# Sliding-window attention in a fused three-block kernel: two key blocks' probabilities in one 128x128 tile

## The chip, the cores and the metric

One core of a Trainium2 chip runs one program. The metric is device microseconds (us) of one execution, as the median of several. The engines are named as in the profile: PE is TensorE's matrix product, PEld its weight load, DVE is VectorE, ACT ScalarE, POOL GpSimd, SP SyncE.

## The reference, cut to what matters

The program is three transformer blocks in a row on 512 tokens of width 1024. The change is in the second block's mixer, an attention in which each 128-query block sees its own key block and the one before it, but only the last 128 keys:

```python
rel = QBLK + a_idx - j_idx                 # a: query in its block, j: key in the 256 of two blocks
def block(args):
    ...
    valid = (rel >= 0) & (rel < C_WINDOW) & (key_pos >= 0)     # C_WINDOW = 128
    bias = jnp.where(valid, alibi, MASK_VALUE)                 # -slope * rel, or -1e30
    s = jnp.einsum('bqhgd,bkhd->bhgqk', qi, kb) * scale + bias
    m = jnp.maximum(jnp.max(s, axis=-1, keepdims=True), sink)
    p = jnp.exp(s - m)
    denom = jnp.sum(p, axis=-1, keepdims=True) + jnp.exp(sink - m)
    return jnp.einsum('bhgqk,bkhd->bqhgd', p / denom, vb)
```

There are 16 query heads of 64 columns on 2 key/value heads. Query a of a block sees key j of its own block where j <= a, and key j of the block before where j > a. So of every two keys with the same number j exactly one is seen.

## The kernel before

Everything is fp32, products of activations and weights are made of three products of rounded parts (hi and lo). `c_stage` of each engine holds the second mixer. It takes the 16 heads as 8 pairs (m = 0, 1 is the head in the pair) and each pair in two rounds r of two query blocks (b = 0, 1; i = 2(r % 2) + b is the query block), 16 rounds in all. Every engine runs its own instruction stream in the written order, and they meet by semaphores only. The order of work is a loop over r in each engine's `c_stage`, with 18 iterations, since the steps of a round are spread over three of them:

- PE, iteration r: `scores(r)` (products of queries and keys to PSUM), `fill(r)` (12 of the products of the next projection's weights, line 1295, which need nothing of the attention), `turn(r-1)` (transposes of the probability tiles of the round before, line 1355), every second iteration a small product for the query norm, and `values(r-2)` (line 1372, transposed probabilities against the value tokens `vtok`).
- DVE, iteration r: `finish(r-1)` (line 2304 takes the reciprocal of the row sums, line 2309 multiplies the tiles by it, in place, and releases `turn` by `c_fin`), `maxima(r)` (line 2295: negative score plus bias into the probability tile, and its row minimum), in odd iterations `scaled` (line 2273, the queries of the next pair, on which the next `scores` waits), in even ones `output` (line 2320, the low part of the finished head pair), then evacuations of `fill`'s banks and `lo_piece` (line 2249, the low part of the weights that `fill` uses later).
- ACT, iteration r: the norm's logarithm and exponential in odd iterations (`norm_job`), or `high` (line 1704) in even ones, `exps(r)` (line 1691, four exponentials with row sums, one for each head and query block), `copy(r-1)` (line 1700, transposed tiles from PSUM to SBUF), `hi_piece` (line 1661, the high part of weights), and in four iterations `square_high` (line 1682).

Two of the waits cross the loops. `lo_piece`'s first half waits until both halves of `hi_piece` are done, and the second of these stands in the same iteration (r = 1, 5, 11, 15), behind `copy(r-1)`. `square_rest` (line 2316, DVE, at the head of iterations 1, 5, 7 and 11) waits for `square_high`, which stands at the end of ACT's iteration before.

A probability tile is 320 columns wide in memory: 256 of keys (block i-1, then block i; for i = 0 only the second 128 are used) and one column with the sink's negative logit, which the exponential adds to the row sum. The lines that the change touches in `turn` and `values`:

```python
for b, i, w in c_blocks(r):                # w = 128 for i = 0, else 256
    for j in range(256 - w, 256, P):
        last = pe.transpose(psum[:, 6 + m, 256 * b + j:256 * b + j + P], c_prob(m, r, b)[:, j:j + P], ident)
```

So `turn` makes 6 transposes for an even round and 8 for an odd one, and `values` one product for each seen key block, head and query block: 14 for a pair (each shows as two records).

## Time and profile before

| what | us |
|---|---|
| median of 3 runs | 1877.54 (1877.28 to 1877.8) |
| the profiled execution | 1877.37 |
| its span on the core | 1875.6 |
| the attention rounds, 578.4 to 680.0 of the span | 101.6 |

The page gives busy time for each engine and the chain of work that ended last. In a timeline row the first number is the start in the span, the second the time from the start of the row's first instruction to the end of its last; a row may hold several instructions (x8) that overlap. What stands in square brackets is how long the engine had sat idle before and what ended that. Instruction durations overlap the next one's start a little, so four in a row take less than four times one.

### The profile page before, as it was taken

How to read it: one execution, taken by the hardware profiler on the slowest of the kernel's cores; microseconds unless marked ns; L12 is line 12 of the kernel's file. 1: busy time of each engine (PE TensorE's matmuls, PEld its weight loads, DVE VectorE, ACT ScalarE, POOL GpSimd, SP SyncE). 2: the span in 40 equal slices, each digit the busy share in tenths (PEclk: the TensorE clock that was granted, in tenths of full speed). 3: DMA queues.
4: the chain of work that ended last, by engine and by line, in shares of the span. 5: the costliest groups of instructions: out<-in, count | busy, mean ns of one | idle time of the engine just before them, and what ended most of it. 6: DMA issues, size and time to landing. Idle time of an engine off the chain costs nothing.

```text
span 1875.6 us, 24415 instructions
## 1 busy us (share of the span) xinstructions
PE 1861.8 (99%) x8998; PEld 1497.4 (80%) x8998; DVE 1189.6 (63%) x1841; ACT 794.4 (42%) x1197; POOL 148.0 (8%) x108
## 2 busy tenths in 40 slices
PE   8999999999999999999999999999999999999999
PEld 6767888888887788888888887888777788888887
DVE  5786677357647866763566498675666667743762
ACT  5365443133435754342334343422577544322441
POOL 2022000000021010000000101121211010000000
PEclk9999999999999999999999999999999999999999
DMA  6212222322231122223232322435333122223222
GB/s 218 70 62 70 92 89 76 114 102 89 84 106 57 51 85 90 89 90 112 90 103 74 125 90 92 142 131 181 137 130 113 68 91 89 80 99 113 90 78 101
DMA packets 39105, 185.99 MB, mean 99 GB/s; under 512 B 4416, under 2 KB 5312, under 8 KB 24432
## 3 DMA queue, kind: packets, MB, share of 16 engines
q1 hardware_dynamic: 38736, 184.77, 28.8%
q8 instruction: 49, 0.80, 0.2%
q14 instruction: 32, 0.26, 0.0%
q10 hardware_dynamic: 288, 0.16, 0.0%
HBM read 176.42 MB, written 8.49 MB: 99 GB/s over the span
## 4 chain that ended last, share of the span: by engine, by line
PE 94%; DVE 4%; ACT 1%; issue 0%; DMA 0%; DVEq 0%; SPq 0%; ACTq 0%
PE banks L760 55%; PE banks L1295 22%; PE banks L807 5%; PE banks L837 1%; PE banks L1209 1%; PE banks L1234 1%; PE banks L1220 1%; PE banks L1343 1%; DVE w_lo L1996 1%; PE banks L1372 1%; DVE tmp L2390 1%; PE banks L1355 1%; PE banks L1308 1%; ACT w_hi L1449 1%; PE banks L969 1%
## 5 line engine op out<-in xcount | busy, mean ns | idle before, releaser
L760 PE MATMUL banks<-xn_hi,w_hi 128*128 128x512 f32 x1208 | 468.4, 391 | 0.2 <-DVE big L2088 0.2
L760 PE MATMUL banks<-xn_hi,w_lo 128*128 128x512 f32 x1208 | 466.1, 389 | 0.0
L760 PE MATMUL banks<-xn_lo,w_hi 128*128 128x512 f32 x1208 | 466.0, 389 | 0.0
L1449 ACT ACTIVATE w_hi<-raw 128x2048 fp32r<-128x2048 f32 (+2 forms) x134 | 228.3, 1703 | 228.4 <-PE banks L760 190.0
L1996 DVE TENSOR_TENSOR w_lo<-raw,w_hi 128x2048 fp32r<-128x2048 f32 (+2 forms) x134 | 273.6, 2042 | 48.5 <-ACT w_hi L1449 48.0
L760 PEld LDWEIGHTS banks<-xn_hi,w_hi 128*128 128x128 f32 x1208 | 226.7, 188 | 49.1 <-issue 1.8
L760 PEld LDWEIGHTS banks<-xn_lo,w_hi 128*128 128x128 f32 x1208 | 226.8, 188 | 48.0 <-issue 1.2
L760 PEld LDWEIGHTS banks<-xn_hi,w_lo 128*128 128x128 f32 x1208 | 226.7, 188 | 47.4
L1511 ACT ACTIVATE tmp<-scaled_h,par 128x512 f32<-128x512 f32 x132 | 100.6, 809 | 349.9 <-DVE scaled_h L2046 349.8
L2046 DVE TENSOR_TENSOR scaled_h<-banks,token_rs 128x512 f32<-128x512 f32 x132 | 85.1, 686 | 186.2 <-PE banks L760 165.9
L1295 PE MATMUL banks<-xn_hi,w_hi 128*128 128x512 f32 x400 | 161.2, 403 | 0.6 <-DVE big L2096 0.6
L1295 PE MATMUL banks<-xn_lo,w_hi 128*128 128x512 f32 x400 | 158.8, 397 | 0.0
L1295 PE MATMUL banks<-xn_hi,w_lo 128*128 128x512 f32 x400 | 158.6, 396 | 0.0
L760 PE MATMUL banks<-hid_hi,w_hi 128*128 128x512 f32 x396 | 154.0, 389 | 0.0
L760 PE MATMUL banks<-hid_lo,w_hi 128*128 128x512 f32 x396 | 154.0, 389 | 0.0
L760 PE MATMUL banks<-hid_hi,w_lo 128*128 128x512 f32 x396 | 154.0, 389 | 0.0
L2019 DVE TENSOR_TENSOR x<-banks,x 128x512 f32<-128x512 f32 (+1 forms) x47 | 32.5, 692 | 169.1 <-PE banks L760 150.9
L659 POOL TENSOR_TENSOR sq<-sq 128x512 f32<-128x512 f32 x38 | 58.4, 1538 | 845.2 <-ACT sq L1455 833.7
L2054 DVE SCALAR_TENSOR_TENSOR tmp<-scaled_h,par,tmp 128x511 f32<-128x511 f32 x132 | 98.8, 748 | 34.9 <-ACT tmp L1511 34.9
L2058 DVE SCALAR_TENSOR_TENSOR tmp<-scaled_h,par,tmp 128x510 f32<-128x510 f32 x132 | 99.1, 750 | 14.5 <-DVE tmp L2054 12.4
L2249 DVE TENSOR_TENSOR w_lo<-raw,w_hi 128x1024 fp32r<-128x1024 f32 (+2 forms) x59 | 81.2, 1379 | 38.4 <-ACT w_hi L1661 38.4
L1295 PEld LDWEIGHTS banks<-xn_hi,w_hi 128*128 128x128 f32 x400 | 75.1, 188 | 28.8 <-issue 13.3
(288 smaller groups left out, 2626.4 us busy)
## 6 DMA issues: line engine op xcount, KB each, us to landing
raw<-weights SPq DMA_DIRECT2D x114, 1024.0 KB, 4.8
raw<-weights SPq DMA_DIRECT2D x24, 768.0 KB, 4.4
raw<-weights SPq DMA_DIRECT2D x24, 640.0 KB, 3.9
big<-scratch SPq DMA_DIRECT2D x40, 256.0 KB, 4.4
att<-scratch SPq DMA_DIRECT2D x16, 256.0 KB, 4.3
scratch<-stage SPq DMA_DIRECT2D x12, 256.0 KB, 4.4
scratch<-con SPq DMA_DIRECT2D x12, 256.0 KB, 2.2
raw<-weights SPq DMA_DIRECT2D x5, 512.0 KB, 3.8
```

The source lines that it names most:

```text
L659: pool.tensor_tensor(chunk(sq, 0), chunk(sq, 0), chunk(sq, c), ALU.add).then_inc(sq_summed, 1)
L760: return pe.matmul(psum[:, 2 * p + m, :], w[:, at_:at_ + P], x_part(k), start=start, stop=stop)
L807: return pe.matmul(psum[:, 2 * (s % 2), :], w[:, at_:at_ + P], x_part(k), start=(k == 0 and t == 0), stop=(k == k_n - 1 and t == 2))
L1295: ins = pe.matmul(c_bank(u), w[:, at_:at_ + P], x_part(k), start=(k == 0 and t == 0), stop=(k == k_n - 1 and t == 2))
L1449: act.activation(w_hi[:, sl], raw[:, sl], ACT.Identity).then_inc(hi_done, 1)
L1511: act.activation(chunk(tmp, 2 * j + m), chunk(scaled_h, 2 * j + m), ACT.Identity, bias=pcol(conv_b, c), scale=pcol(conv, 3 * c + 2)).then_ ...
L1996: dve.tensor_tensor(w_lo[:, sl], raw[:, sl], w_hi[:, sl].bitcast(F32), ALU.subtract).then_inc(lo_done, 1)
L2019: last = dve.tensor_tensor(chunk(x, c), psum[:, 2 * ((a + j) % 2) + m, :], chunk(x, c), ALU.add)
L2046: dve.tensor_tensor(chunk(scaled_h, 2 * j + m), psum[:, 2 * ((a + j) % 2) + m, :], token_rs[:, :], ALU.mult).then_inc(h_scaled, 1)
L2054: me.mark(dve.scalar_tensor_tensor(out=chunk(tmp, t, 1), in0=bank[:, 0:T - 1], scalar=pcol(conv, 3 * c + 1), in1=chunk(tmp, t, 1), op0=ALU ...
L2058: dve.scalar_tensor_tensor(out=chunk(tmp, t, 2), in0=bank[:, 0:T - 2], scalar=pcol(conv, 3 * c), in1=chunk(tmp, t, 2), op0=ALU.mult, op1=A ...
L2249: ins = dve.tensor_tensor(w_lo[:, sl], raw[:, sl], w_hi[:, sl].bitcast(F32), ALU.subtract)
```

## The change

The two key blocks' scores of one query block are put into one 128-column tile by an elementwise minimum (the tile holds negative scores, and a masked key has +1e30, so the minimum picks the seen one of each two keys): `c_pack`, line 2321 in the new file, for the query blocks with i > 0. The exponential, the division and the transpose then work on 128 columns each. In the transposed tile the rows j <= a belong to the own block. The product with the values becomes: whole tile times the values of the block in front, plus (tile times the triangle mask `tri`) times the difference of values between the own block and the one in front. The differences are computed once (`v_diff`, line 2363) before the rounds; the masked copy once a round and head (`masked`, line 2333), behind the rest of DVE's iteration. For i = 0 only the whole tile times the own block's values is needed.

The division moves from DVE to ACT (`normed`, line 1706), at the head of ACT's iteration; DVE keeps the reciprocal.

```diff
         def c_prob(m, r, b):
             return att[:, bass.ds(7 * T + 320 * (4 * (r % 2) + 2 * b + m), 320)]
+        v_diff = chunk(att, 3)
+        def c_packs(r, m, b):
+            return 6 * (r // 2) + (m + 1 if r % 2 == 0 else 2 + 2 * m + b + 1)
...
-                        for b, i, w in c_blocks(r):
-                            for j in range(256 - w, 256, P):
-                                last = pe.transpose(psum[:, 6 + m, 256 * b + j:256 * b + j + P], c_prob(m, r, b)[:, j:j + P], ident)
+                        for b in range(2):
+                            last = pe.transpose(psum[:, 6 + m, b * P:(b + 1) * P], c_prob(m, r, b)[:, P:2 * P], ident)
                         last.then_inc(c_pt, 1)
...
                     pe.wait_ge(c_copied, 2 * r + 2)
+                    pe.wait_ge(c_masked, 2 * r + 2)
                     for b, i, w in c_blocks(r):
-                        first = max(i - 1, 0)
-                        for j in range(first, i + 1):
+                        parts = [(vtok[0], max(i - 1, 0), b * P)] + ([(v_diff, i - 1, (2 + b) * P)] if i else [])
+                        for n, (v, j, from_) in enumerate(parts):
                             for m in range(2):
                                 at_ = j * P + 64 * m
-                                from_ = 256 * b + 256 - w + (j - first) * P
-                                last = pe.matmul(psum[64 * m:64 * m + 64, 2, i * P:(i + 1) * P], vtok[0][:, at_:at_ + 64],
+                                last = pe.matmul(psum[64 * m:64 * m + 64, 2, i * P:(i + 1) * P], v[:, at_:at_ + 64],
                                                  c_slot(m, r)[:, from_:from_ + P],
...
                 def exps(r):
-                    n = 4 * r
                     for m in range(2):
                         for b, i, w in c_blocks(r):
-                            n += 1
-                            act.wait_ge(c_max, n)
-                            pr = c_prob(m, r, b)[:, 256 - w:257]
+                            if i:
+                                act.wait_ge(c_pack, c_packs(r, m, b))
+                            else:
+                                act.wait_ge(c_max, 4 * r + 2 * m + 1)
+                            pr = c_prob(m, r, b)[:, P:2 * P + 1]
...
+                def normed(r):
+                    act.wait_ge(c_inv, r + 1)
+                    for m in range(2):
+                        for b, i, w in c_blocks(r):
+                            pr = c_prob(m, r, b)[:, P:2 * P]
+                            last = act.activation(pr, pr, ACT.Identity, scale=row_inv[:, 2 * i + m:2 * i + m + 1])
+                        last.then_inc(c_fin, 1)
+
                 def copy(r):
...
-                        act.activation(c_slot(m, r)[:, c0:T], psum[:, 6 + m, c0:T], ACT.Identity).then_inc(c_copied, 1)
+                        act.activation(c_slot(m, r)[:, 0:2 * P], psum[:, 6 + m, 0:2 * P], ACT.Identity).then_inc(c_copied, 1)
...
                 for r in range(C_ROUNDS + 2):
+                    if 1 <= r <= C_ROUNDS:
+                        normed(r - 1)
...
+                    for m in range(2):
+                        dve.wait_ge(c_max, 4 * r + 2 * m + 2)
+                        for b, i, w in c_blocks(r):
+                            if i:
+                                pr = c_prob(m, r, b)
+                                dve.tensor_tensor(pr[:, P:2 * P], pr[:, 0:P], pr[:, P:2 * P], ALU.min).then_inc(c_pack, 1)
 
                 def finish(r):
                     n = 4 * (r % 2)
                     dve.wait_ge(c_exp, 4 * r + 4)
-                    me.mark(dve.reciprocal(row_inv[:, n:n + 4], row_sum[:, n:n + 4]))
-                    me.wait()
+                    dve.reciprocal(row_inv[:, n:n + 4], row_sum[:, n:n + 4]).then_inc(c_inv, 1)
+
+                def masked(r):
+
+                    b0 = 1 - r % 2
                     for m in range(2):
-                        for b, i, w in c_blocks(r):
-                            pr = c_prob(m, r, b)[:, 256 - w:256]
-                            last = dve.tensor_scalar(pr, pr, row_inv[:, 2 * i + m:2 * i + m + 1], None, ALU.mult)
-                        last.then_inc(c_fin, 1)
+                        dve.wait_ge(c_copied, 2 * r + m + 1)
+                        dve.tensor_tensor(c_slot(m, r)[:, (2 + b0) * P:T].rearrange("p (j l) -> p j l", j=2 - b0),
+                                          c_slot(m, r)[:, b0 * P:2 * P].rearrange("p (j l) -> p j l", j=2 - b0),
+                                          ccol("tri", 0, P).rearrange("p (o l) -> p o l", o=1).to_broadcast([P, 2 - b0, P]), ALU.mult).then_inc(c_masked, 1)
...
+                dve.wait_ge(c_v, 1)
+                dve.tensor_tensor(v_diff[:, 0:3 * P], vtok[0][:, P:T], vtok[0][:, 0:3 * P], ALU.subtract).then_inc(c_v, 1)
                 for r in range(C_ROUNDS + 2):
...
                             lo_piece(s + 1, r - g0 - 1, 2)
+                    if 1 <= r <= C_ROUNDS:
+                        masked(r - 1)
```

The change also moves instructions. DVE at the end of iteration 11 and the start of iteration 12, before (lines 2295, 2273, 2277, 2264, 2249, 2304, 2309 are the maxima, the next queries, the bias, an evacuation, the low part of weights, the reciprocal, the division):

```order
L2295 ISA att,small<-banks,att,small 128x256
L2295 ISA small 128x1
L2273 SCALAR_TENSOR_TENSOR att<-big,small,rsk 128x512
L2277 TENSOR_SCALAR att<-con 128x256
L2264 TENSOR_TENSOR x<-banks,x 128x512
L2249 TENSOR_TENSOR w_lo<-raw,w_hi 128x1024
L2304 RECIPROCAL small<-small 128x4
L2309 TENSOR_SCALAR att<-att,small 128x256 x4
```

The same place in the changed program (2321 is the pack, 2265 the low part of weights, 2333 the masked copy):

```order
L2311 ISA att,small<-banks,att,small 128x256
L2311 ISA small 128x1
L2321 TENSOR_TENSOR att<-att 128x128 x4
L2289 SCALAR_TENSOR_TENSOR att<-big,small,rsk 128x512
L2293 TENSOR_SCALAR att<-con 128x256
L2280 TENSOR_TENSOR x<-banks,x 128x512
L2265 TENSOR_TENSOR w_lo<-raw,w_hi 128x1024
L2333 TENSOR_TENSOR att<-att,con 128x128 x2
L2326 RECIPROCAL small<-small 128x4
```

Four packs now stand between the maxima and the next pair's queries, two masked copies between the low part and the reciprocal, and the four divisions are gone. ACT at the end of iteration 11, before (1691 the exponentials, 1700 the copies, 1661 the high part of weights, 1704 `high`):

```order
L1691 ACTIVATE att,small<-att,small 128x257 x4
L1700 ACTIVATE att<-banks 128x384 x2
L1661 ACTIVATE w_hi<-raw 128x1024
L1704 ACTIVATE big_r<-banks 128x512
L1691 ACTIVATE att,small<-att,small 128x129
```

And in the changed program (1698 the exponentials, 1714 the copies, 1667 the high part, 1706 the division, 1718 `high`):

```order
L1698 ACTIVATE att,small<-att,small 128x129 x4
L1714 ACTIVATE att<-banks 128x256 x2
L1667 ACTIVATE w_hi<-raw 128x1024
L1706 ACTIVATE att<-att,small 128x128 x4
L1718 ACTIVATE big_r<-banks 128x512
L1698 ACTIVATE att,small<-att,small 128x129 x4
```

The four divisions stand at the head of each iteration, ahead of `high` and the exponentials.

## Rows read from the trace of the kernel before

**Rows 1.** The page: span, and busy time of each engine.

```profile
span 1875.6 us, 24415 instructions
...
PE 1861.8 (99%) x8998; PEld 1497.4 (80%) x8998; DVE 1189.6 (63%) x1841; ACT 794.4 (42%) x1197; POOL 148.0 (8%) x108
```

**Rows 2.** The rounds as one window: PE, PEld, DVE, ACT, POOL busy, clock, DMA.

```profile
578.40:680.00 101.60, 101.51 (x701) 76.98 (x701) 82.76 (x271) 70.55 (x196) 8.40 (x7) 1.00 0.16 53
```

**Rows 3.** Timeline of PE, rounds 4 to 6: starts of scores and of transposes.

```profile
599.53 0.93 PE L1343 MATMUL banks<-att 64*128 64x128 f32 x8
...
605.88 1.14 PE L1343 MATMUL banks<-att 64*128 64x256 f32 x8
...
609.83 0.82 PE L1355 MATMUL banks<-con,att 128*128 128x128 f32 x6
...
611.60 0.93 PE L1343 MATMUL banks<-att 64*128 64x128 f32 x8
```

**Rows 4.** Groups by shape, 540 to 700 us: busy us, mean ns, idle before.

```profile
L1691 ACT ACTIVATE att<-att,small 128x257 f32<-128x257 f32 x48 | 24.0, 502 | 5.1 <-DVE small L2295 5.1
...
L1691 ACT ACTIVATE att<-att,small 128x129 f32<-128x129 f32 x16 | 6.4, 398 | 15.4 <-DVE small L2295 15.4
...
L1671 ACT ACTIVATE lt<-banks,con 128x512 f32<-128x512 f32 x9 | 6.2, 684 | 8.2 <-PE banks L1331 8.2
...
L2295 DVE CUSTOM_DVE_ANT_0 att<-banks,att,small 128x256 f32<-128x256 f32 x48 | 21.2, 479 | 3.7 <-PE banks L1343 3.7
...
L2309 DVE TENSOR_SCALAR att<-att,small 128x256 f32<-128x256 f32 x48 | 14.6, 347 | 0.3
...
L2249 DVE TENSOR_TENSOR w_lo<-raw,w_hi 128x1024 fp32r<-128x1024 f32 x6 | 7.3, 1222 | 6.6 <-ACT w_hi L1661 6.6
...
L2249 DVE TENSOR_TENSOR w_lo<-raw,w_hi 128x512 fp32r<-128x512 f32 x2 | 1.4, 684 | 2.0 <-ACT w_hi L1661 2.0
```

**Rows 5.** Timelines of DVE, ACT and PE, from iteration 1 to the transposes of iteration 2.

```profile
585.93 0.75 DVE L2273 SCALAR_TENSOR_TENSOR att<-big,small,rs 128x512 f32<-128x512 f32 x1
...
587.54 0.87 ACT L1700 ACTIVATE att<-banks 128x384 f32<-128x384 f32 x2 [0.62 <-PE banks L1355]
...
587.76 0.93 PE L1343 MATMUL banks<-att 64*128 64x128 f32 x8
...
589.39 1.23 DVE L2249 TENSOR_TENSOR w_lo<-raw,w_hi 128x1024 fp32r<-128x1024 f32 x1 [2.45 <-ACT w_hi L1661]
...
590.74 1.14 DVE L2309 TENSOR_SCALAR att<-att,small 128x256 f32<-128x256 f32 x4
...
591.48 1.12 PE L1355 MATMUL banks<-con,att 128*128 128x128 f32 x8
```

**Rows 6.** The same timelines, from iteration 11 to the transposes of iteration 12.

```profile
641.97 0.69 DVE L2316 TENSOR_TENSOR tn_r<-tn,more_r 128x512 fp32r<-128x512 f32 x1 [0.58 <-ACT more_r L1682]
...
645.74 0.87 ACT L1700 ACTIVATE att<-banks 128x384 f32<-128x384 f32 x2 [0.55 <-PE banks L1355]
...
647.59 1.23 DVE L2249 TENSOR_TENSOR w_lo<-raw,w_hi 128x1024 fp32r<-128x1024 f32 x1 [1.77 <-ACT w_hi L1661]
...
648.93 1.14 DVE L2309 TENSOR_SCALAR att<-att,small 128x256 f32<-128x256 f32 x4
...
650.70 1.04 PE L1355 MATMUL banks<-con,att 128*128 128x128 f32 x8
```

**Rows 7.** The same timelines, from iteration 15 to the transposes of iteration 16.

```profile
668.78 0.87 ACT L1700 ACTIVATE att<-banks 128x384 f32<-128x384 f32 x2 [0.24 <-PE banks L1355]
...
671.97 1.14 DVE L2309 TENSOR_SCALAR att<-att,small 128x256 f32<-128x256 f32 x4
...
672.88 1.04 PE L1355 MATMUL banks<-con,att 128*128 128x128 f32 x8
```

**Rows 8.** Timeline of POOL and DVE in iteration 4 and 5.

```profile
604.14 1.04 POOL L695 TENSOR_TENSOR tn<-big 128x512 f32<-128x512 f32 x1 [7.81 <-DVE big L2260]
...
604.18 1.80 DVE L2309 TENSOR_SCALAR att<-att,small 128x128 f32<-128x128 f32 x4
```

More of the change, by code:

```diff
@@ L295, in blocks_program @@
         c_turned_v, c_v = sem("c_turned_v"), sem("c_v")
+        c_pack, c_inv, c_masked = sem("c_pack"), sem("c_inv"), sem("c_masked")
         c_scored, c_max, c_exp, c_fin = sem("c_scored"), sem("c_max"), sem("c_exp"), sem("c_fin")
@@ L1361, in values @@
                         if it == 0:
-                            pe.wait_ge(c_v, 1)
+                            pe.wait_ge(c_v, 2)
                         else:
@@ L1365, in values @@
                     pe.wait_ge(c_copied, 2 * r + 2)
+                    pe.wait_ge(c_masked, 2 * r + 2)
                     for b, i, w in c_blocks(r):
-                        first = max(i - 1, 0)
-                        for j in range(first, i + 1):
+                        parts = [(vtok[0], max(i - 1, 0), b * P)] + ([(v_diff, i - 1, (2 + b) * P)] if i else [])
+                        for n, (v, j, from_) in enumerate(parts):
                             for m in range(2):
                                 at_ = j * P + 64 * m
-                                from_ = 256 * b + 256 - w + (j - first) * P
-                                last = pe.matmul(psum[64 * m:64 * m + 64, 2, i * P:(i + 1) * P], vtok[0][:, at_:at_ + 64],
+                                last = pe.matmul(psum[64 * m:64 * m + 64, 2, i * P:(i + 1) * P], v[:, at_:at_ + 64],
                                                  c_slot(m, r)[:, from_:from_ + P],
-                                                 start=(i == 0), stop=(i == 3 and j == 3), skip_group_check=True)
+                                                 start=(i == 0), stop=(i == 3 and n == 1), skip_group_check=True)
                     last.then_inc(c_pv, 1)
@@ L1684, in exps @@
                 def exps(r):
-                    n = 4 * r
                     for m in range(2):
                         for b, i, w in c_blocks(r):
-                            n += 1
-                            act.wait_ge(c_max, n)
-                            pr = c_prob(m, r, b)[:, 256 - w:257]
+                            if i:
[3 more added lines that the diff above has]
+                            pr = c_prob(m, r, b)[:, P:2 * P + 1]
                             act.activation(pr, pr, ACT.Exp, scale=-1.0, bias=neg_max[:, 2 * i + m:2 * i + m + 1],
                                            accum_out=row_sum[:, 2 * i + m:2 * i + m + 1]).then_inc(c_exp, 1)
+                def normed(r):
[5 more added lines that the diff above has]
+                        last.then_inc(c_fin, 1)
                 def copy(r):
-                    c0 = P if r % 2 == 0 else 0
                     for m in range(2):
```

## The prediction, on record before the run

> **What bounds the kernel now.** I read the page first: PE is busy for 1861.8 of 1875.6 us [rows 1]. Then the window of the attention rounds: in 101.6 us PE is busy for 101.5, at a granted clock of 1.00, while DVE has 82.8 and ACT 70.6 [rows 2]. So PE sets the time here, and what the change is worth is PE's work saved less the new waits on PE's path. DVE and ACT matter only where they make PE wait. DVE at 81% has little room, so I looked at the timelines for the places where its work only just arrives in time. Beyond the stage PE is bound in the same way, so I pass a gain or loss of this stage to the end one to one.
>
> **What PE loses and gains.** Rounds alternate: 8 transposes take 1.04 us from the first start to the last end [rows 7], 6 take 0.82 [rows 3], so one more costs 0.11. The change makes 4 in each round: 2 fewer in each of 8 even rounds, 4 fewer in each of 8 odd ones, 48 in all. 48 x 0.11 = **5.3 us saved**, the most that the change can give. `values` keeps its 14 products a pair, scores and `fill` are untouched. PE's iterations get shorter: the one from 599.53 to 605.88 held 8 transposes (6.35 becomes 5.9), the one from 605.88 to 611.60 held 6 (5.7 becomes 5.5) [rows 3].
>
> **What DVE loses and gains.** Gone: four divisions a round, four of 256 columns in 1.14 us [rows 5], starts 0.265 apart. New: packs, 2 in even and 4 in odd rounds, and two masked copies a round. No row shows a two-input operation of 128 columns. 512 columns take 0.684 and 1024 take 1.222 [rows 4], 1.05 ns a column, so 128 columns are 0.28 long and, with 0.08 of overlap with the next as the divisions show, 0.20 apart. The ends for it are 0.13 (its columns alone) and 0.35 (a 256-column division, 0.347 [rows 4]); I take 0.20. A masked copy of 256 columns is then 0.33 apart. An odd round: 0.8 of packs, 0.4 of masked copies (it masks the even round before) for 1.0 removed; an even one: 0.4 and 0.66 for 1.1. DVE's total hardly moves (+0.1 a round), its order does. `v_diff` adds one operation of about 0.45 before the rounds; its cover is DVE's idle time before the first scores, all but some 0.15.
>
> **What ACT loses and gains.** Four divisions a round of 128 columns. The nearest row is the exponential of 129 columns with a per-row operand, 0.398 [rows 4]: 0.40 long and about 0.29 apart (I take off the 0.09 to 0.1 by which consecutive activations overlap: two copies take 0.87 [rows 5]); ends 0.2 and 0.4. Four are 1.2 us, the first two ready after 0.29 + 0.40 = 0.69. Exponentials shrink from 257 to 129 columns, 0.50 to 0.40 [rows 4], copies by 0.1 to 0.2 each at the same slope. Net for a pair about +0.5 us; ACT had 31 us free in the window [rows 2].
>
> **The new latency.** Before, the first exponential could start after the first maximum. Now it waits for the fourth one and a pack, since the packs stand behind all four maxima: 3 x (0.48 - 0.08) + 0.20 = +1.4 us, of which the shorter exponentials give back 4 x 0.1. Then the copy, which stands behind the exponentials, and then the masked copies, which stand behind the copy and *behind `lo_piece`*, with the reciprocal of the next iteration queued behind them on DVE, on which ACT's division and PE's transposes wait. That ring (reciprocal 0.2, division 1.2, norm 1.3, which is two activations of 512 columns of 0.68 and the like [rows 4], or `high`, one of them, exponentials 1.6, copies 0.65, masked 0.5 to 0.7) is about 5.4 us in an odd and 4.8 in an even iteration, against PE's 5.5 and 5.5 to 5.9: it fits in an ordinary iteration, narrowly. Where it does not fit is where `lo_piece` waits for the `hi_piece` of the same iteration, so that both (about 1.0 and 1.15) stand in the ring: iterations 1, 11, 15. In iteration 5 the pieces are half as wide and I find over 1 us left.
>
> - **Iteration 1 to 2.** Before, the first two divided tiles were ready at 590.74 + 0.27 + 0.35 = 591.35 and PE came at 591.48 [rows 5]: 0.1 to spare. Now: +1.4 (maxima and pack), +0.4 (the maxima themselves start later, as ACT's first exponentials also wait for packs and `square_rest` stands behind them), -0.4, -0.6 (the copy had waited 0.62 for PE [rows 5]), -0.2 (narrower copies), +0.5 (masked, with a hop), +0.1 (division on ACT) = +1.2. PE itself comes 0.1 later (two transposes less, but see next), so it waits 0.9; then for the other head, whose two divisions need 0.58 while PE's two transposes need 0.22, 0.36 more. And `scores(2)` waits for the next queries: they ended at 586.68 [rows 5], 1.1 before the scores at 587.76; +0.4 and +0.8 of packs, with PE 0.2 earlier, give 0.3. Together **1.6**.
> - **Iteration 11 to 12.** `square_rest` at 641.97 was already waiting for ACT [rows 6]; against PE it comes about 1.3 later now, as ACT's iteration 10 ends 0.8 later and PE's is 0.44 shorter. +1.3, +1.4, -0.4, -0.55 [rows 6], -0.2, +0.5, +0.1 = +2.1, against 650.70 less (648.93 + 0.62) = 1.15 to spare [rows 6]: 0.95, and 0.36. Then 0.25 at the next scores, and `values` waits about 0.3 for `output` of the same iteration. **1.9**.
> - **Iteration 15 to 16.** +1.4, -0.4, -0.24 [rows 7], -0.2, +0.5, +0.1 = +1.15, against 672.88 less (671.97 + 0.62) = 0.3 to spare, with PE 0.2 earlier: 1.05, and 0.36. **1.4**.
>
> **Contention, weighed apart.** POOL's square at 604.14 took 1.04, and four divisions beside it 1.80 instead of about 1.0 [rows 8]: one of them stood still. That goes with the divisions, but it lay where DVE had room, so I book nothing. The Trainium skill (SBUF — State Buffer, section "Who interferes with whom") says that a VectorE instruction with two SBUF inputs also contends with a GpSimd instruction that reads SBUF, and that the later one fully blocks. The trace agrees as to the one-input form; none of its rows shows a pack. By that rule a masked copy in iterations 4, 6, 8 and 10 would stand still for up to one square, 1.0 us; I find these iterations with slack enough, so the sum would stay.
>
> **Sum.** -5.3 + 1.6 + 1.9 + 1.4 = -0.4 us on the profiled 1877.37, which is within 0.2 of the median 1877.54. **Forecast 1877.1.** The bounds of the unknown prices move the waits: at 0.13 a pack and 0.2 a division each of the three places is 0.6 to 0.8 shorter (waits 2.8, time 1875.0); at 0.35 and 0.4 each is 0.9 longer and iterations 6, 10 and 13 begin to wait (waits 8.5, time 1880.7).
>
> **Rivals.**
> - *Cheap ring: all of the gain arrives.* If less than 1.5 us of waits come (the copies and masks finish before I think, since DVE's 19% of free time absorbs them), the time is 1877.5 - 5.3 + 0 to 1.5 = 1872.2 to 1873.7. For it: PE has nearly no waits today. Against it: the 0.1 and 0.3 us to spare in rows 5 and 7, which any added latency uses up. Chance 0.10.
> - *The ring binds everywhere: slower.* If a pack costs 0.35, a division 0.4 and every hop between engines another 0.05, the ring grows by about 0.7 in each iteration and passes PE's 5.5 in the odd ones; a pair then costs 11.9 instead of 11.4. Six ordinary pairs give 3.0, the three places 9.0: -5.3 + 12 = +6.7, 1884. The point from which it decides is a ring of 5.7 us on the mean. For it: DVE at 81%, and three more crossings between engines a round than before. Against it: the rows of similar operations. Chance 0.13.
> - *The transposes were not PE's pace.* If weight loads and not the count set it, the gain is smaller than 5.3. The 0.22 between 8 and 6 [rows 3, 7] speaks against it; it lies inside the range.
>
> **Chances.** Forecast's case 0.77, cheap ring 0.10, binding ring 0.13. About 0.2% (3.75 us) is what a measurement of this kernel can tell from no change. Faster by more needs waits below 1.5: 0.10. Slower by more needs waits above 9: the binding ring and the upper edge of the forecast's case, 0.14. The range of 1873.9 to 1881.2 holds the bounds of the prices, leaves out most of the first rival and the upper part of the second.
>
> **What would show it.** In the profile after: 64 records of transposes, four in about 0.6 us; PE idle ahead of the transposes of iterations 2, 12 and 16, about 0.9 to 1.3 us each, released by ACT's division; PE rounds of about 5.5 between. Wrong would be: no such idle time (first rival), idle time ahead of every odd round's transposes or scores (second), or a division or pack far from 0.40 and 0.28. If PE's idle time sits elsewhere, my walk through the iterations was wrong though the sum may hold.

## The result, and the profile after it

The changed kernel takes 1881.52 us (median; 1879.54 to 1882.28 over 19 runs), the kernel before 1877.55 beside it. The ratio is 1.002, with a 95% interval from 1.0013 to 1.0026: 4 us slower. The forecast was 1877.1 and its range ended at 1881.2. The two profiled spans stand 4.2 us apart, 1875.6 and 1879.8. The page of the changed kernel, against [rows 1]:

```profile
span 1879.8 us, 24408 instructions
...
PE 1858.3 (99%) x8950; PEld 1491.1 (79%) x8950; DVE 1192.6 (63%) x1858; ACT 801.9 (43%) x1261; POOL 149.5 (8%) x108
```

PE has 48 instructions fewer and is busy 3.5 us less, yet the span is longer. So most of the loss is PE's idle time. I cut each trace at two points: the start of the first scores, and the end of the last values. Before the first point nothing moved. Between them lie the rounds, and behind the second the rest. The rounds of the kernel before, which [rows 2] show in a slightly wider window, and those of the changed one (window, PE, PEld, DVE, ACT, POOL busy, clock, DMA):

```profile
578.42:678.69 100.27, 100.18 (x696) 75.89 (x695) 82.13 (x270) 69.29 (x194) 8.38 (x7) 1.00 0.15 49
```

```profile
578.52:680.93 102.41, 96.73 (x648) 70.38 (x647) 84.27 (x287) 76.62 (x258) 8.64 (x7) 1.00 0.14 48
```

The rounds are 2.1 us longer, with PE idle for 5.7 us where it was idle for 0.1. The rest is 1875.6 - 678.7 = 1196.9 before and 1879.8 - 680.9 = 1198.9 after, **2.0 us longer**, in code that the change does not touch. The two together are the whole difference.

**Prices.** Groups by shape, 575 to 690 us, against [rows 4]: exponentials, divisions on ACT, packs, copies, wide masked copies.

```profile
L1698 ACT ACTIVATE att<-att,small 128x129 f32<-128x129 f32 x64 | 24.9, 392 | 7.6 <-DVE small L2311 4.8 <-DVE att L2321 2.7
...
L1706 ACT ACTIVATE att<-att,small 128x128 f32<-128x128 f32 x64 | 20.5, 391 | 14.7 <-DVE small L2326 14.7
...
L2321 DVE TENSOR_TENSOR att<-att 128x128 f32<-128x128 f32 x48 | 11.0, 284 | 0.0
...
L1714 ACT ACTIVATE att<-banks 128x256 f32<-128x256 f32 x32 | 10.1, 365 | 0.0
...
L2333 DVE TENSOR_TENSOR att<-att,con 128x256 f32<-128x256 f32 x16 | 9.7, 643 | 1.5 <-ACT att L1714 1.5
```

**Waits.** What PE's weight loads waited for in the same stretch (total, times, longest), where the kernel before had 1.1 us in four waits besides issue:

```profile
PEld banks L1361 <- ACT att L1706: 3.8, 6, 0.9
...
PEld banks L1350 <- DVE att L2289: 2.3, 5, 0.7
PEld banks L1378 <- DVE big_r L2345: 2.3, 4, 1.0
PEld banks L1302 <- DVE w_lo L2265: 1.6, 2, 1.3
PEld banks L1302 <- DVE big_r L2345: 1.1, 1, 1.1
```

L1361 is the transposes, L1350 scores (for the next queries), L1378 values and L1302 the fill (for `output` and for `lo_piece`). Weight loads run ahead of the products, so these 11.1 us are more than PE lost (the products' own waits with a name come to 5.2). The loss in the rounds is the difference: 2.1 + 5.3 saved = **7.4 us**. Where it arises shows from the starts of the scores, before and after, when 0.11 us is added back for each transpose saved: 0.4 in iteration 1, 1.0 in 2, 0.5 in 3, 0.3 in 7, 1.95 in 10, 0.2 in 11, 1.3 in 12, 1.8 from the start of 15 to the end of the last values, and less than 0.05 in every other.

**The dearest place** was not among my three. Iteration 10 took 7.85 us where it took 6.34, although it has four transposes less (starts of scores 634.30 and 642.15; before 634.91 and 641.25). DVE, then ACT, then PE's weight loads:

```profile
633.79 2.28 DVE L2265 TENSOR_TENSOR w_lo<-raw,w_hi 128x2048 fp32r<-128x2048 f32 x1
635.99 0.49 DVE L2333 TENSOR_TENSOR att<-att,con 128x128 f32<-128x128 f32 x2
636.39 0.17 DVE L2326 RECIPROCAL small<-small 128x4 f32<-128x4 f32 x1
...
638.39 0.69 DVE L2345 TENSOR_TENSOR big_r<-banks,big_r 128x512 fp32r<-128x512 f32 x1 [1.77 <-ACT big_r L1718]
```

```profile
636.60 1.28 ACT L1706 ACTIVATE att<-att,small 128x128 f32<-128x128 f32 x4 [1.70 <-DVE small L2326]
637.78 0.58 ACT L1718 ACTIVATE big_r<-banks 128x512 fp32r<-128x512 f32 x1
```

```profile
636.13 0.30 PEld L1302 LDWEIGHTS banks<-big_r,w_hi 128*128 128x128 f32 x2 [1.31 <-DVE w_lo L2265]
...
639.14 0.30 PEld L1302 LDWEIGHTS banks<-big_r,w_hi 128*128 128x128 f32 x2 [1.10 <-DVE big_r L2345]
```

Read it as a chain. The low part of the weights, 2.28 us long, and the masked copies stand ahead of the reciprocal on DVE. The divisions wait for the reciprocal on ACT. `high`, whose input had been ready since values at 634, waits behind the divisions. DVE's `output` waits for `high`, and PE's fill for `output`.

### The profile page after: what moved, and what is told of

It reads as the page before. It is cut to its first block, busy times and chain, and to the rows that moved or that the text cites. A ratio compares the mean times of both kernels' runs of the same rounds, so it can differ in the third digit from the quotient of the medians.

```text
span 1879.8 us, 24408 instructions
## 1 busy us (share of the span) xinstructions
PE 1858.3 (99%) x8950; PEld 1491.1 (79%) x8950; DVE 1192.6 (63%) x1858; ACT 801.9 (43%) x1261; POOL 149.5 (8%) x108
## 4 chain that ended last, share of the span: by engine, by line
PE 87%; DVE 6%; ACT 4%; issue 2%; DMA 0%; POOL 0%; SPq 0%; DVEq 0%; ACTq 0%; POOLq 0%
PE banks L767 55%; PE banks L1302 19%; PE banks L814 5%; PE banks L1241 1%; PE banks L1216 1%; PE banks L1227 1%; ACT att L1698 1%; DVE w_lo L2265 1%; DVE w_lo L2012 1%; DVE tmp L2419 1%; DVE att L2311 1%; ACT w_hi L1667 1%; PE banks L1315 1%; ACT w_hi L1455 1%; PE banks L976 1%
## 5 line engine op out<-in xcount | busy, mean ns | idle before, releaser
L1302 PE MATMUL banks<-xn_hi,w_hi 128*128 128x512 f32 x400 | 161.2, 403 | 0.6 <-DVE big L2112 0.6
L1302 PE MATMUL banks<-xn_lo,w_hi 128*128 128x512 f32 x400 | 158.8, 397 | 0.0
L1302 PE MATMUL banks<-xn_hi,w_lo 128*128 128x512 f32 x400 | 158.5, 396 | 0.0
L1302 PEld LDWEIGHTS banks<-xn_hi,w_hi 128*128 128x128 f32 x400 | 75.0, 188 | 28.9 <-issue 12.9
```

The source lines that it names most:

```text
L1302: ins = pe.matmul(c_bank(u), w[:, at_:at_ + P], x_part(k), start=(k == 0 and t == 0), stop=(k == k_n - 1 and t == 2))
```

## Experiments

All figures below that are called rounds and rest are cut at the same two points of each profiled run, one run of each kernel. The start of the rounds, which the table leaves out, lay at 578.0 to 578.7 us, but at 577.7 in e5 and at 579.4 in e9.

| kernel | median us | rounds | rest |
|---|---|---|---|
| before | 1877.5 | 100.3 | 1196.9 |
| changed | 1881.5 | 102.4 | 1198.9 |
| e1 before, half the transposes | 1873.96 | 96.8 | 1196.8 |
| e2 before, 20 transposes more | 1879.69 | 102.5 | 1196.9 |
| e3 masked copies later | 1886.69 | 108.5 | 1198.9 |
| e4 division on DVE | 1888.04 | 108.8 | 1198.9 |
| e5 before, 17 DVE instructions more | 1877.46 | 100.4 | 1196.9 |
| e6 reciprocal first | 1879.81 | 100.7 | 1198.9 |
| e7 packs by head | 1881.53 | 102.5 | 1198.9 |
| e8 order in the third block | 1880.76 | 102.4 | 1198.0 |
| e9 changed, 20 transposes more | 1881.09 | 103.4 | 1196.8 |
| e10 before, 32 transposes fewer | 1875.58 | 97.7 | 1197.9 |
| e11 e6 and `high` first | 1877.51 | 98.4 | 1198.8 |
| e12 squares on ACT | 1882.68 | 104.5 | 1199.0 |
| e13 changed, 48 transposes more | 1881.68 | 104.3 | 1197.0 |
| e14 e11, 20 tiny products | 1876.89 | 99.3 | 1197.0 |
| e15 e14, packs by head | 1877.01 | 99.7 | 1196.9 |

### What the transposes are worth, and what the chain costs

```
-    for j in range(256 - w, 256, P):
+    for j in range(P, 256, P):
```

> The kernel before with only the transposes changed: each round turns the second 128 columns of each of its four probability tiles and leaves the first block of the two-block tiles unturned, so 48 transposes fewer and part of the result is not computed; nothing else differs. Theory (PE's count sets the pace): 48 x 0.11 us = 5.3 us less, 1872.2 us. Rival (transposes are not PE's pace, weight loads or the engines behind them are): less than 2.5 us less, 1875 or more.

Measured 1873.96 (ratio 0.9982, 0.9972 to 0.9991), 3.5 us less. This lies between the two. The count does hold: e2 added 20 transposes and the rounds grew by 2.2, 0.11 each. But with the old chain behind it PE, which now arrives earlier, waits for DVE at once, in iterations 2, 3, 12 and at the end, and 5.3 - 3.5 = **1.8 us** go there.

The opposite run keeps the new chain and gives PE its old work back:

```
-    for b in range(2):
+    for b in [0, 1] + [0, 1] * (r % 2) + [1] * (r % 2 == 0):
```

> The changed kernel with its transposes done again up to the count of the kernel before (6 in an even and 8 in an odd round, 48 more, same data and place), so that PE's iterations are as long as before and only the new chain differs. PE's program is then as long as before too, so the time behind the rounds should be 1196.9. Theory (the chain costs waits of its own, and the shorter iterations of PE expose the rest: the kernel before with half the transposes gained only 3.5 of 5.3 us): the rounds take 1 to 3.5 us more than the 100.3 of the kernel before, 1878.5 to 1881 us. Rival A (the chain fits under PE's old pace): the rounds take within 0.5 of 100.3, 1877.5 to 1878. Rival B (the chain's waits are the same at either pace): the rounds take 102.4 + 5.3 = 107.7, 1885 us.

Measured 1881.68, rounds 104.3: the chain alone costs **4.0 us** at PE's old pace, a little more than the theory's bound, and neither rival holds. The window rows of e1 and e13:

```profile
578.19:674.96 96.77, 95.43 (x648) 70.59 (x647) 81.99 (x270) 68.92 (x194) 8.38 (x7) 1.00 0.15 51
```

```profile
578.12:682.41 104.29, 101.71 (x696) 75.60 (x695) 84.09 (x287) 77.34 (x258) 8.64 (x7) 1.00 0.14 47
```

So 1.8 and 4.0 of the 7.4 arise from each alone, and 1.6 only from both together.

### Which part of the chain

```
-    (end of DVE's iteration r)   if 1 <= r <= C_ROUNDS: masked(r - 1)
+    (behind alibi in iteration r)   if r >= 2: masked(r - 2)
```

> The changed kernel with the masked copies of round r issued on VectorE in iteration r+2 (behind its maxima, packs and next biases, ahead of the evacuations) instead of at the end of iteration r+1. Theory (the masked copies that stood still beside GpSimd's square, five pairs of 1.2 to 1.6 us instead of 0.75, and their wait for ScalarE's copies, delay the next reciprocal and the next maxima): some 2 to 3 us of the waits of 7.4 us go, and they take 0.75 a pair: 1878.5 to 1879.5 us. Rival (the waits come from the chain maxima, packs, exponentials, reciprocal, division on ScalarE, whatever stands at the end of VectorE's iteration): 1881 to 1882 us.

Measured 1886.69, 5 us worse than the changed kernel. I had put `masked(r - 2)` into the iteration in which `values(r - 2)` reads it, behind the next queries. Timeline of DVE, then of PE:

```profile
610.52 0.75 DVE L2289 SCALAR_TENSOR_TENSOR att<-big,small,rs 128x512 f32<-128x512 f32 x1
...
611.44 0.76 DVE L2333 TENSOR_TENSOR att<-att,con 128x256 f32<-128x256 f32 x2
```

```profile
612.35 0.88 PE L1378 MATMUL banks<-att 128*64 128x128 f32 x12 [1.01 <-ACT att L1714]
```

The wait is put down to ACT's copy, which had long been done; the masked copies ended at 612.20. The waits ahead of the transposes fell all the same, from 3.8 to 1.5. That fits copies that had delayed the reciprocal, but PE was also later here, so this run alone doesn't show it. Part of the 5 us may be the clock. PE's longest wait for values there, 1.92 us, ends at 651.16, and in the two windows after it starts the granted clock fell below 1.00:

```profile
650.00:653.00 3.00, 1.84 (x16) 1.56 (x16) 2.60 (x6) 1.98 (x7) 0.00 (x0) 0.71 0.00 0
653.00:656.00 3.00, 3.00 (x16) 2.12 (x15) 1.54 (x10) 2.26 (x7) 0.00 (x0) 0.72 0.00 0
```

Each is a mean over the two levels, 2.4 GHz (1.00) and 1.2 GHz (0.50). That is 3 x 0.29 + 3 x 0.28 = 1.7 us of full clock at most, the only such place in that run's rounds.

```
     finish(r - 1)
+    masked(r - 2)
     sink_columns, maxima(r) ...
-    masked(r - 1) at the end of the iteration
```

> The changed kernel with VectorE's order at the turn of an iteration exchanged: the reciprocal of round r-1 comes ahead of the masked copies of round r-2, both ahead of the maxima of round r. The masked copies are then 5 us earlier than in the run that had them behind the next queries. Theory (masked copies that stand ahead of the reciprocal delay it, and with it ScalarE's division and the transposes): of the 3.8 us ahead of the transposes some 2 go, values keeps its waits, 1879.5 to 1880.5 us. Rival (what the reciprocal gains the maxima pay, since they still stand behind both): 1881.5 us within 0.5.

Measured 1879.81, 1.7 us less than the changed kernel: the theory's number. It came from the transposes (weight loads' waits 3.8 to 2.6, less than the 2 us said), and also from scores (2.3 to 1.8) and the fill (2.7 to 1.7). Two of its ten runs were 1.7 us shorter still, 1878.0 and 1878.2; why stays open.

```
+    if r % 2 == 0 and r >= 4: high(r // 2 - 2)
     if 1 <= r <= C_ROUNDS: normed(r - 1)
-    if r % 2 == 0 and r >= 4: high(r // 2 - 2)
```

> The kernel of the run with the reciprocal first, and ScalarE's high copy ahead of the divisions in the even iterations. In iteration 10 of that run high began at 636.5, 2.9 us behind the last product that it reads, because it stood behind the divisions; VectorE's output waited 1.4 us for it, the maxima behind that, and PE's fill and values waited 0.7 and 2.2 us for outputs. Theory (that order is a cause of its own of PE's waits): 1.5 to 2 us less than the 1879.8 of that run, 1878 us. Rival (the divisions, now 0.6 later, make the transposes wait as much longer): 1879.5 to 1880 us.

Measured 1877.51, 2.3 us less again, a little more than expected. In iteration 10 `high` now runs as soon as values is done, and `output` no longer waits. ACT, then DVE:

```profile
633.76 0.60 ACT L1718 ACTIVATE big_r<-banks 128x512 fp32r<-128x512 f32 x1
...
635.21 1.28 ACT L1706 ACTIVATE att<-att,small 128x128 f32<-128x128 f32 x4 [0.85 <-DVE small L2326]
```

```profile
635.54 0.68 DVE L2345 TENSOR_TENSOR big_r<-banks,big_r 128x512 fp32r<-128x512 f32 x1
```

Iteration 10, which had lost 1.95 us in the changed kernel and 1.2 in e6, lost 0.7 here; iteration 12 went from 1.3 to 0.6 and the end, from 15 on, from 1.4 (e6) to 0.55. So 4.0 of the 7.4 us were two instructions behind others that did not need to be ahead of them.

```
-    four maxima, then the packs of both heads
+    per head: its two maxima, then its packs
```

> The changed kernel with the packs of the first head issued behind the maxima of the first head, instead of behind all four maxima. The exponentials of the first head can start 2 x 0.40 = 0.8 us earlier. Theory (the longer way from the maxima to the divided tiles, 1.4 us, makes the waits ahead of the transposes): it shrinks by 0.8 in each round, 3 of the 7.4 us of waits go, 1878.5 us. Rival (ScalarE still waits for the second head's packs, which come as late as before, so its last exponential ends no earlier): under 1 us, 1880.5 to 1881.5.

Measured 1881.53, the rival. Iteration 2 lost 0.4 us less than in the changed kernel, but 3 and 7 lost 0.7 more between them. The likely reason, argued from one place and not tested: ACT does not wait for the packs where it is fullest. In iteration 3 of the changed kernel the exponentials follow division and norm without a gap:

```profile
597.23 1.28 ACT L1706 ACTIVATE att<-att,small 128x128 f32<-128x128 f32 x4 [2.00 <-DVE small L2326]
598.42 0.67 ACT L1677 ACTIVATE lt<-banks,con 128x512 f32<-128x512 f32 x1
599.18 0.63 ACT L1681 ACTIVATE rsk<-lt 128x512 f32<-128x512 f32 x1
599.72 0.39 ACT L1698 ACTIVATE att<-att,small 128x129 f32<-128x129 f32 x1
```

```
+    (DVE, finish) four dve.tensor_scalar(pr, pr, row_inv, None, ALU.mult), c_fin
-    (ACT) normed(r - 1)
```

> The changed kernel with the four divisions of 128 columns of each round left on VectorE behind the reciprocal, ScalarE has none. VectorE does them in about 4 x 0.20 = 0.8 us against ScalarE's 1.28, with one crossing between engines less, and ScalarE's high copy and norm no longer stand behind them. Theory (waits for ScalarE's division, 3.8 us ahead of the transposes, and the high copy behind it, 1 to 2 us, are the larger part of the waits): 1.5 to 3 us less, 1878.5 to 1880 us. Rival (VectorE is the fuller engine, 83% before, and 0.8 us more a round make its own waits longer): 1883 us or more.

Measured 1888.04: DVE is busy 97.6 of 108.8 us of the rounds, and scores, values and fill wait for it. At most 1.7 of the 6.5 us more than in the changed kernel are clock (below). So on this kernel the division is better placed on ACT.

### The contention

Wide masked copies beside POOL's square in the changed kernel, and without it:

```profile
594.54 1.95 POOL L702 TENSOR_TENSOR tn<-big 128x512 f32<-128x512 f32 x1 [13.85 <-DVE big L2276]
```

```profile
595.51 1.60 DVE L2333 TENSOR_TENSOR att<-att,con 128x256 f32<-128x256 f32 x2
```

```profile
655.95 0.75 DVE L2333 TENSOR_TENSOR att<-att,con 128x256 f32<-128x256 f32 x2
```

Five of the eight pairs took 1.2 to 1.6 us. By the Trainium skill (SBUF — State Buffer, "Who interferes with whom") a VectorE instruction with two SBUF inputs and a GpSimd one that reads SBUF shut each other out; the trace now agrees for this form too, 0.75 against 1.6.

```
+    (ACT, even r) act.activation(sq[n % 2], chunk(big, n - 1), ACT.Square)   # n = r // 2 + 3
-    (POOL) the squares of n = 3 to 8
```

> The changed kernel with the squares of queries 3 to 8 taken from GpSimd to ScalarE (0.62 us in six even iterations, behind its copies and weight pieces), so that no VectorE instruction of the rounds has GpSimd beside it. Theory (the wide masked copies of 1.2 to 1.6 us instead of 0.75 are VectorE standing still beside GpSimd's squares): every wide pair takes 0.75; 5 x 0.75 us of VectorE's time come back, of which PE gets 1 to 2.5: 1879 to 1880.5 us. Rival (ScalarE's 0.62 more cost as much, or those iterations had slack): 1881 to 1882 us, still with pairs of 0.75; if the pairs stay at 1.2 to 1.6 the reading of the contention was wrong.

Every wide pair took about 0.75, so the reading of the contention was right. The time was 1882.68, 1.2 us *more*. The rival holds: 0.62 us more on ACT in six iterations costs more than the contention did. What the contention alone is worth in time this run cannot say, but it gives a hint: iterations 3 and 7, which had lost 0.5 and 0.3 us and in which the reciprocal stands behind such a pair, lost nothing here. (The 104.5 of the table holds 1.7 us of a lower clock, which this profiled run alone had, below; the other runs were 1.0 to 1.4 us shorter than it.)

### The 2 us behind the rounds

In the attention of the third block POOL's first square starts late and PE waits for it. POOL of before, POOL of after, PE of after:

```profile
1344.95 2.49 POOL L729 TENSOR_TENSOR tn<-big 128x512 f32<-128x512 f32 x2 [10.24 <-DMA big<-scratch]
```

```profile
1348.62 2.67 POOL L736 TENSOR_TENSOR tn<-big 128x512 f32<-128x512 f32 x2 [11.68 <-DMA big<-scratch]
```

```profile
1349.90 1.12 PE L1187 MATMUL banks<-tn,con 128*128 128x512 f32 x2 [1.02 <-POOL tn L736]
```

It is 3.67 later, of which 2.24 is the lateness of the rounds. PE's starts behind the rounds, counted from their end, agree in the two kernels within 0.15 us but for two steps. The first, 1.2 us, is this wait. The second, 0.8 us, follows 11 us later: two of DVE's divisions stand beside POOL's next squares and take 2.12 us (after) where they took 0.75 (before), and PE waits for the maxima behind them. DVE of before, DVE of after, PE of after:

```profile
1355.19 0.75 DVE L2685 TENSOR_SCALAR big<-big,small 128x384 f32<-128x384 f32 x2
```

```profile
1358.37 2.12 DVE L2714 TENSOR_SCALAR big<-big,small 128x384 f32<-128x384 f32 x2
```

```profile
1361.76 0.40 PE L1206 MATMUL banks<-mask_b,ident_b 128*128 128x128 bf16 x4 [0.60 <-DVE small L2701]
```

Three guesses at the cause fell first.

```
-    for j in range(256 - w, 256, P):
+    for j in list(range(256 - w, 256, P)) * (1 if r < C_ROUNDS - 1 else 4 if m else 3):
```

> The kernel before with 20 of the transposes of round 15 done again (same data to the same place), 20 x 0.11 = 2.2 us more of PE at the end of the rounds, as late as the changed kernel is at that point; nothing downstream differs. Theory M (what happens after the rounds depends on the exact time at which they end: the third block's attention starts with VectorE and GpSimd in another order): the third block gives another 2 us, 1881.6 us, and GpSimd's first square there starts behind VectorE's subtractions. Rival C (the extra 2 us in the third block comes from something else that the change leaves behind, or is chance of one run): 1879.7 us and the third block as before.

Rest 1196.9: being late does not do it.

```
+    if r: dve.tensor_copy(qg[:, 0:1], sub_g)
```

> The kernel before with one tiny VectorE copy (one column, into a gain that nothing reads any more) at the start of each of iterations 1 to 17, so that its VectorE program has as many instructions ahead of the third block as the changed kernel's, 17 more; nothing else differs. So far the time from the end of the rounds to the end of the span is 1196.9 us in all three kernels made from the one before (two of them with the rounds 3.7 us earlier and 2.2 us later) and 1198.9 in all three made from the changed one. Theory I (where the longer VectorE program stands when its next instructions are loaded decides whether VectorE or GpSimd goes first in the third block): 1198.9 here too, about 1879.6 us. Rival N (it is something else that the change brings, such as its three new semaphores or its data): 1196.9 and 1877.6 us.

Rest 1196.9, 1877.46 us: the length of DVE's program does not do it.

```
+    dve.wait_ge(f_sq, 3)
     for c in range(4, DC): gated_low(c)
```

> The changed kernel with one wait more, far behind the rounds: in the third block VectorE's four subtractions start only when GpSimd's first square there is done. In the profile of the changed kernel that square started 3.7 us later than in the one before, only 2.2 of them the lateness of the rounds, right behind VectorE's subtractions, and PE then waited 1.0 us for it. Theory (the 2.0 us behind the rounds are GpSimd's square standing still behind VectorE's two-input subtractions): the time behind the rounds goes back from 1198.9 to about 1197, 1879.6 us. Rival (the transfer that the square waits for comes later by itself): 1198.9 or more, 1881.5 us or more.

Rest 1198.0, half of it back: PE's first wait shrank from 1.02 to 0.55 us and the second did not arise. But the square started at 1348.35, still 1.1 too late with no subtraction beside it. So its *transfer* was late by itself. Then I looked at what shares the DMA engines with it. The queues and the transfers issued in a window of 5.8 us that starts 662.3 us behind the end of the rounds, of before and of after (last number: us from issue to landing):

```profile
q1 hardware_dynamic: 416, 1.44, 61.9%
q14 instruction: 1, 0.01, 0.3%
issues: line engine op xcount, KB each, median us to landing
big<-scratch SPq DMA_DIRECT2D x1, 256.0 KB, 2.9
```

```profile
q1 hardware_dynamic: 416, 1.44, 62.2%
q8 instruction: 1, 0.02, 1.2%
q14 instruction: 1, 0.01, 0.3%
issues: line engine op xcount, KB each, median us to landing
big<-scratch SPq DMA_DIRECT2D x1, 256.0 KB, 4.3
```

The same transfer lands after 4.3 instead of 2.9 us, and a packet of an instruction load on queue 8 is new in that window. Counted from the end of the rounds this packet lay at 655.8 us before, 669.0 in e1 (48 PE instructions fewer), 651.4 in e2 (20 more), 655.3 in e5 (17 DVE instructions more), and 665.0 in the changed kernel.

```
+    for b in [0, 1] * (6 if r == C_ROUNDS - 1 else 1):
```

> The changed kernel with 20 of the transposes of round 15 done again (same data, same place), 2.2 us more of PE. In all kernels made from the changed one a packet of the instruction loads on DMA queue 8 lies at 664.5 to 665.5 us behind the end of the rounds, between the issue (663.3) and the landing (666.2 before, 667.5 after) of the transfer that GpSimd's first square of the third block waits for; in the kernels made from the one before it lies at 655 or 668 and moves with the number of PE's instructions (48 fewer: 13 us later; 20 more: 4 us earlier), not with VectorE's. Theory P (that load is PE's program, and it holds up the transfer): with 20 instructions more it comes some 4 to 5 us earlier, at about 660, the transfer lands in time, the time behind the rounds is 1196.9: 1881.5 + 2.2 - 2.0 = 1881.7 us. Rival N (something else in the changed kernel): 1198.9 and 1883.7 us.

```
+    for j in range(256 - w if r > 10 else P, 256, P):
```

> The kernel before with 32 transposes left out (the first block of the two-block tiles of rounds 0 to 10 is not turned, part of the result is not computed). 48 fewer put the packet of instruction loads at 668 us behind the rounds; with 16 instructions more than that it should come 3.7 us earlier, at 664 to 665, where the changed kernel has it. Theory P (that load is PE's program and holds up the third block's transfer): 1198.9 us behind the rounds in a kernel that has nothing of the change, 2.4 us saved in the rounds, 1877.2 us. Rival N: 1196.9 and 1875.2 us.

Theory P predicted both signs. e9 has 2 us *more* PE work than the changed kernel and is no slower (1881.09), rest 1196.8, packet at 661.2. e10 has nothing of the change, packet at 664.9, rest 1197.9: 1.0 of the 2.0 us, PE's first wait without the second, and its median was 1875.58, between the two expectations. Landing times in e9, then in e10:

```profile
big<-scratch SPq DMA_DIRECT2D x1, 256.0 KB, 3.2
```

```profile
q8 instruction: 1, 0.02, 1.0%
...
big<-scratch SPq DMA_DIRECT2D x1, 256.0 KB, 4.1
```

Over all seventeen profiles the two go together, and so does the landing: in the nine with the packet at 664.7 to 665.1 (the changed kernel, e3, e4, e6, e7, e8, e10, e11, e12) the transfer lands after 4.0 to 4.3 us and the rest is 1197.9 to 1199.0, in the other eight it lands after 2.8 to 3.3 and the rest is 1196.8 to 1197.0. How one packet delays a transfer of 256 KB by over a microsecond is not shown.

### A version with both

```
+    if r == C_ROUNDS - 1:      # ahead of the transposes, ten per head
+        pe.matmul(psum[0:1, 6 + m, 0:1], ident[:, 0:1], c_prob(m, r, 0)[:, P:P + 1], start=True, stop=True)
```

> The kernel of the run with high first (1877.5 us, 1198.8 us behind the rounds) with 20 tiny products of one row and one column ahead of the transposes of round 15, which the transposes overwrite. They put PE's program at the length of the run that added 20 transposes to the changed kernel, where the load on queue 8 came at 661 us behind the rounds and the time behind them was 1196.8. Theory P: 1196.9 behind the rounds, 20 x 0.03 to 0.1 us more in them: 1876.1 to 1877.5 us, faster than the kernel before by up to 1.4. Rival (the load's place alone does not decide): 1878 us or more.

> The same with the packs of the first head behind the maxima of the first head. On the changed kernel alone this gave nothing (1881.5), where the masked copies and high still stood in ScalarE's and VectorE's way. Theory (with these out of the way the 0.8 us earlier exponentials reach PE): 0.5 to 1 us less than the run without it. Rival (the last exponential sets the reciprocal, and it comes no earlier): the same within 0.3 us.

e14: 1876.89 (ratio 0.9997, 0.9988 to 1.0006), rest 1197.0 as expected; the packet was at 655.3, not at 661. The expectation had the length wrong: the 20 tiny products show as 40 products and 40 weight loads, the 20 transposes of e9 as 20 and 20. Counted that way the changed kernel's PE has 96 records fewer than the kernel before and 16 waits more, 80 fewer together; e14 gives these 80 back, and its packet stands where the kernel before has it, at 655.8. So e14 agrees with the theory that the length of PE's program places the packet. e15: 1877.01, no gain from the packs. Both lie 0.6 us below the kernel before beside them, which these runs do not tell from no change.

## Why the prediction was wrong

- **What bounds the kernel**, PE: right.
- **48 x 0.11 = 5.3 us saved**: right as a count and as a price (e2). Left out was that some of it cannot arrive even with the old chain, 1.8 us (e1). I had read that PE has nearly no waits and the small margins, and used them only for the new latency, not for PE's own earlier arrival in every iteration.
- **Prices**: right. Pack 0.284 (taken 0.28), division 0.391 and four in 1.28 (0.40, 1.2), exponential 0.392 (0.40), four transposes in 0.6. The price that was off is the wide masked pair, 1.2 to 1.6 in five of eight cases where I had 0.7.
- **The waits, 4.9 us at three places and nothing elsewhere: this term of the sum failed, it measured 7.4.** The three places came as told, 1.4, 1.55 and 1.8 us where I had 1.6, 1.9 and 1.4, together 4.8. For the transposes of iterations 2, 12 and 16 I had 0.9 + 0.36, 0.95 + 0.36 and 1.05 + 0.36; PE's weight loads waited 0.93 + 0.38, 0.85 + 0.39 and 0.82 + 0.38. Too small was the end: values at 676.09 waited 0.77, where I had nothing. What failed is the "nothing elsewhere": 2.7 us, of them 1.95 in iteration 10, which I had found to have slack enough, and 0.5 and 0.3 in iterations 3 and 7, where scores waited for the next queries. In iteration 10 PE's products waited 0.91 for the low part of the weights and 0.68 for `output`. I had looked for trouble where `lo_piece` waits for its `hi_piece`, and not where it is 2.28 us long and stands between the exponentials and the reciprocal. And I counted `high` as part of the ring, not as an instruction with an early input and an urgent reader that the division would stand in front of.
- **The latency of +1.4 from packs behind the maxima**: the size was right for a lone round (in iteration 1 the first exponential started 0.53 behind the first maximum before and 1.94 after), but taking 0.8 of it away left the time as it was (e7).
- **Contention booked at nothing**: probably too low, by the 0.5 and 0.3 us of iterations 3 and 7, which were gone in e12. That run changed ACT's order too, and in e6 the loss of 0.3 was gone although the contention stayed, so this is not proven.
- **"I pass a gain or loss of this stage to the end one to one"**: failed, by 2.0 us, and the runs give its cause: a packet of the instruction load beside one transfer of the third block. Without these 2.0 us the time would have been about 1879.5, inside the range.
- **The rival of the ring that binds everywhere** came nearest in sign, but its mechanism did not occur: iterations 5 and 6 lost nothing (rounds 5 to 7 began at 605.88, 611.60 and 617.55 before, at 606.56, 612.03 and 617.55 after). A few iterations lose much.

Sum: -5.3 + 7.4 + 2.0 = +4.1, against 4.0 between the medians.

## What to carry to other kernels

In this kernel PE has no idle time and the engines behind it have a few tenths to spare, and a third of the PE work removed (1.8 of 5.3 us) was given back at once; in such a kernel measure the ceiling first by leaving the work out. Compare the starts of the same step, iteration by iteration, before and after: it shows at once which iterations lose. When a step moves to another engine, list what now stands behind it there and ask of each whether its input is early and its reader urgent: two exchanges of that kind were worth 4 of 7.4 us. And a small difference that arises in untouched code can be real and repeatable: compare the length of that code in several variants before explaining it.

## What the hardware showed that I had not expected

- The place of an instruction load matters. A packet of 16 KB (49 of them are 0.80 MB) beside a transfer of 256 KB went with a landing time of 4.0 to 4.3 us instead of 2.8 to 3.3, and with 1.0 to 2.0 us at the end. The Trainium skill (Runtime: NRT & Kernel Launch, "Instruction fetch mechanics") says that the program is fetched in blocks of 16 KiB and that crossing one is mostly hidden. The trace agrees as to the size; as to hidden, PE's starts behind the rounds agree in the kernels before and changed but for the two waits shown, so no load is seen to stop PE there, but the transfer beside it was not spared.
- The clock can fall behind PE's waits. Behind 1.92 us of waiting in e3 it was granted at 0.71 and 0.72 in two windows of 3 us, and in e4 at 0.75 and 0.69 in the window with a wait of 1.54 and the next, while a wait of 1.62 in the same run, ahead of the scores at 602.17, left it at 1.00. In e12 it was 0.55 and 0.88 behind a window in which PE was busy for 1.68 of 3 us:

```profile
674.00:677.00 3.00, 1.68 (x17) 1.03 (x16) 1.51 (x3) 2.00 (x7) 0.00 (x0) 1.00 0.02 5
677.00:680.00 3.00, 3.00 (x11) 2.29 (x9) 2.18 (x4) 0.00 (x0) 0.00 (x0) 0.55 0.23 46
```

  The changed kernel has the same two waits there (0.40 and 0.77) and kept 1.00, so in these runs it is a risk and no fixed price. None of the 7.4 us is clock.
- The changed kernel's runs spread over 2.7 us, from 1879.54 to 1882.28, those of the kernel before over 1.1. Why stays open; no profile shows one of its shorter runs.
